# Output projections of the token mixers: the first two weight panels multiplied together, their last k tile at the end of both

## The reference, cut to what matters

```python
h = rmsnorm(x, g_norm1[l]) * (1.0 + mod[:, 1]) + mod[:, 0]
out, ctx_tensors = token_mixer(l, h, ctx)      # ends in: o.reshape(b, s, ...) @ w_o
x = x + mod[:, 2] * out
h = rmsnorm(x, g_norm2[l]) * (1.0 + mod[:, 4]) + mod[:, 3]
x = x + mod[:, 5] * swiglu(h, w_ffn_in[l], w_ffn_out[l])
```

## Time and profile before

| | |
|---|---|
| median of three timed runs | 3585.4 us |
| profiled execution, its own time | 3581.15 us |
| span of the profiled execution | 3579.3 us |
| TensorE matmuls busy | 3350.8 us (94%) |
| VectorE busy | 1886.4 us (53%) |
| ScalarE busy | 1123.7 us (31%) |
| mean granted TensorE clock | 0.950 of full speed |

### The profile page before, as it was taken

How to read it: one execution, slowest core, us unless ns; L and a number is a source line. 1 busy time by engine, 2 the same in 40 slices (tenths; PEclk the granted TensorE clock), 3 DMA queues, 4 the chain that set the end, 5 groups by cost and what they waited for, 6 DMA issues and landing times.

```text
span 3579.3 us, 53824 instructions
## 1 busy us (share of the span) xinstructions
PE 3350.8 (94%) x20800; PEld 3121.8 (87%) x20800; DVE 1886.4 (53%) x2732; ACT 1123.7 (31%) x1729; POOL 116.9 (3%) x72
## 2 busy tenths in 40 slices
PE   7899999999989998899999789989999897899999
PEld 7877789999987776799999666789999897899999
DVE  2333355767355665575853445566663687533333
ACT  2344423211134554321111333232111376321111
POOL 0211000000000000000000210000000000000000
PEclk6899998999999999899999899989999998999999
DMA  5211125343221110163522110143532221222222
GB/s 177 61 51 39 38 71 181 125 158 125 75 72 42 42 41 17 47 203 118 184 75 70 55 30 13 47 156 114 177 111 69 66 59 52 60 75 72 76 76 76
DMA packets 451128, 304.16 MB, mean 85 GB/s; under 512 B 12483, under 2 KB 430918, under 8 KB 451014
## 3 DMA queue, kind: packets, MB, share of 16 engines
q1 hardware_dynamic: 440676, 293.75, 26.8%
q10 hardware_dynamic: 10338, 8.88, 0.8%
HBM read 298.49 MB, written 4.10 MB: 85 GB/s over the span
## 4 chain that ended last, share of the span: by engine, by line
PE 85%; DVE 5%; ACT 5%; issue 2%; DVEq 1%; DMA 1%; ACTq 1%; SPq 0%
PE psB L309 30%; PE psA L309 30%; PE psD L309 8%; PE psC L372 3%; PE psA L353 2%; PE psC L325 2%; PE psC L364 2%; PE psB L353 2%; PE psD L826 2%; PE psA L811 1%; ACT h_hi L1459 1%; ACT work L1456 1%; ACTq L1458 1%; DVE work L2362 1%; PE psC L838 0%
## 5 line engine op out<-in xcount | busy, mean ns | idle before, releaser
L1477 ACT ACTIVATE w_hi<-raw 128x1024 fp32r<-128x1024 f32 (+1 forms) x309 | 319.4, 1035 | 1158.1 <-PE psB L309 770.5
L2011 DVE TENSOR_TENSOR w_lo<-raw,w_hi 128x1024 fp32r<-128x1024 f32 (+1 forms) x309 | 367.9, 1192 | 348.5 <-ACT w_hi L1477 348.2
L309 PE MATMUL psA<-h_hi,w_hi 128*128 128x320 f32 x1616 | 383.1, 319 | 46.8 <-DVE h_lo L2085 42.0
L309 PE MATMUL psB<-h_hi,w_hi 128*128 128x320 f32 x1616 | 371.4, 311 | 12.8 <-DVE w_lo L2369 12.8
L309 PE MATMUL psA<-h_lo,w_hi 128*128 128x320 f32 x1616 | 376.3, 315 | 0.0
L309 PE MATMUL psA<-h_hi,w_lo 128*128 128x320 f32 x1616 | 375.0, 314 | 0.0
L309 PE MATMUL psB<-h_lo,w_hi 128*128 128x320 f32 x1616 | 370.8, 311 | 0.0
L309 PE MATMUL psB<-h_hi,w_lo 128*128 128x320 f32 x1616 | 370.5, 311 | 0.0
L309 PEld LDWEIGHTS psA<-h_hi,w_hi 128*128 128x128 f32 x1616 | 274.5, 192 | 62.3 <-issue 32.2
L2041 DVE SCALAR_TENSOR_TENSOR work<-work,silu_c 128x1024 f32<-128x1024 f32 x252 | 312.6, 1282 | 11.7
L309 PEld LDWEIGHTS psB<-h_hi,w_hi 128*128 128x128 f32 x1616 | 272.6, 190 | 14.4 <-DVE w_lo L2369 14.4
(11 more groups left out here) (295 smaller groups left out, 5277.6 us busy)
## 6 DMA issues: line engine op xcount, KB each, us to landing
raw<-in_w_ffn_in SPq DMA_DIRECT2D x176, 512.0 KB, 3.9
work<-in_w_mod SPq DMA_DIRECT2D x144, 512.0 KB, 4.9
raw<-in_w_ffn_out SPq DMA_DIRECT2D x64, 512.0 KB, 4.0
raw<-in_w_ffn_out SPq DMA_DIRECT2D x32, 384.0 KB, 3.3
raw<-in_diff_w_in SPq DMA_DIRECT2D x24, 512.0 KB, 3.8
work<-in_w_mod SPq DMA_DIRECT2D x8, 1024.0 KB, 5.3
raw<-in_w_mod SPq DMA_DIRECT2D x16, 512.0 KB, 4.0
tables<-in_w_mod SPq DMA_DIRECT2D x16, 512.0 KB, 4.4
```

What stands on the lines that cost most here:

```text
L309: last = nc.tensor.matmul(out[:, b, 0:half], w[slot][:, kt * cols + c0:kt * cols + c0 + P], r[:, o:o + half], start=(kt == 0 and p == 0), ...
L1477: nc.scalar.activation(w_hi[s][:, 0:n], raw[s][:, 0:n], ACT.Copy).then_inc(hi_done, 1)
L2011: nc.vector.tensor_tensor(w_lo[s_][:, 0:n], raw[s_][:, 0:n], w_hi[s_][:, 0:n].bitcast(F32), ALU.subtract).then_inc(split_done, 1)
```

## The change

TensorE's instruction list changes in the four calls of `project` for the mixers' projections; the first turn is taken out of the loop and written as `first_pair`. It waits for the splits of both panels, multiplies k tiles 0 to 6 of panel 0 into psA, then k tiles 0 to 6 of panel 1 into psB, waits for the last head's output, and then multiplies k tile 7 of panel 0 and k tile 7 of panel 1. `gemm_done` is counted after each panel's last product, as before. The loop runs over the turns 1 to 3. The instruction lists of VectorE, ScalarE and SP stay as they are.

```diff
-            def project(name, kts, last_source, mod=None):
+            def project(name, kts, last_source, mod=None, mixer=False):
...
+                def first_pair():
+                    for j in range(2):
+                        assert take_panel(pe, name, 0, j) == j
+                    pe.wait_ge(x_done, base)
+                    for part in (range(kts - 1), range(kts - 1, kts)):
+                        if part[0]:
+                            last_source()
+                        for j in range(2):
+                            last = products(pe, psum[j], j, kts, P, 0, act_hi, act_lo, 0, T, TH, part)
+                            if part[0]:
+                                last.then_inc(gemm_done, 1)
+
                 if mod:
                     turn(0)
                     mod_turn(*mod, 2)
-                with pe.Fori(1 if mod else 0, KT // 2) as i:
+                if mixer:
+                    first_pair()
+                with pe.Fori(1 if mod or mixer else 0, KT // 2) as i:
                     turn(i)
...
-                project(f"wo{layer}", KT, lambda: mixed.wait_turns(pe, KT))
+                project(f"wo{layer}", KT, lambda: mixed.wait_turns(pe, KT), mixer=True)
```

## The result

The changed kernel takes 3609.7 us (median of five runs, 3608.43 to 3614.09) against 3585.4 us before on the same chip (five runs, 3583.77 to 3593.97): ratio 1.0065, 95% interval 1.005 to 1.008. It is slower by 24.3 us. Its profiled execution took 3610.07 us, 28.9 more than that of before.

The account below looks back on a forecast made before the run. TensorE, holding 85% of the chain that ended last, was taken to bound the kernel. 15.16 (stalls) + 1.22 (later starts) + 6.52 (clock) - 0.91 (gain) = +22.0 us, from 3585.4 to about 3607; range 3598.5 to 3613.

Parts of the forecast that it names:

- the gain: Fourth projection only: the wait before k tile 7 for the last block's low part goes, saving 0.91 us.
- The stall: Before panel 2 in each projection: TensorE waits 3.79 us for VectorE's `w_lo`, +15.16 us in all.
- Both splits first: Starts of second and fourth projection: 1.14 us later each, costing 0.61 us each at low clock, +1.22 us.
- rival C: Clock falls longer behind stalls (first half); later start delays the second projection's clock rise (second half); +27.3 us, 3613, chance 0.11.
- The clock: Behind each new stall: TensorE's clock falls, losing 1.63 us per stall, +6.52 us.
- Rival B: Behind the stalls: they occur but the clock stays up; +15.5 us, 3601, chance 0.16.
- D: Low-clock stretches behind norms and projection starts: the clock pays the stalls back; +4.2 us, 3590, no change, chance 0.05.

Follow-up runs that it names:

- two k tiles ahead: Changed kernel with only two of panel 1's k tiles before panel 0's last, panel 1's split awaited only ahead of panel 1: -4.2 us against before, ratio 0.9993.
- four k tiles left: Four of panel 1's k tiles drawn ahead of panel 0's last, four following, otherwise like the two-tile kernel; waits 0.98 to 0.99 us, one run only.
- the filler: Changed kernel plus 22 matmuls on unread data between the pair and panel 2 of each mixer's projection: +18.4 us against before, ratio 1.0051.
- the low part first: Changed kernel with VectorE making the next panel's low part after the addition, ahead of the squares, in every turn: +18.9 us against before, ratio 1.0049.
- the old order: Peeled first turn with panel 0 whole, then panel 1, but both splits awaited before the first matmul: +3.8 us against before, ratio 1.0007.
- the late split: Changed kernel with panel 1's split awaited only ahead of panel 1's first product: +15.6 us against before, ratio 1.0047.

## Why the prediction was right

*What bounds it, and the gain.* TensorE's idle time counted in full, and the waits that the change aimed at were covered in three of four places. The 0.91 us of the fourth were got back, also by the kernel with two k tiles ahead.

*The stall.* Forecast 3.79 us per projection from VectorE's 4.53, the 0.14 of the start and the 0.88 of cover. Counted as there, from one matmul's start to the next, it is 2309.38 less 2305.31 + 0.293, 3.78 us. As the profile counts idle time it is 3.62, since a matmul's record reaches 0.17 us past its successor's start. The order in VectorE's list (3.6 to 1.8 us) and the size of the cover (0.98 us with four k tiles left) show that this is the mechanism. One stall per projection and no second came, as argued. The term of 15.16 us was right to 0.1.

*Both splits first.* Forecast 0.61 us twice. In the fourth the later start was paid for as forecast: with the stall, 1.25 + 3.82 = 5.1 us against 3.79 + 1.63 + 0.61 - 0.91 = 5.1. In the second the start came 1.1 us later and the stretch behind it did not shrink by the half that the sum counted on, because the rise of the clock moved along. Counted as start and low clock together, against the first profile of before, this place cost 2.1 and 1.0 us in the two profiles of the changed kernel, 1.0 with the filler, 0.8 with the low part first and 2.0 with the old order. The term was undersized by 0.2 to 1.5 us there, by rival C's second half.

*The clock.* Forecast 1.63 us per stall. It fell behind every one of the 13 waits of 3.6 us in the four profiles that have them. The loss was 1.64 where it is read above, of which 0.11 are the first pair's (in the forecast's 1.63 too, by the same rows), and the filler took out 1.5. In two of the 13 it stayed low for longer and cost 2.7 and 2.5 us in place of 1.5, rival C's first half: the second projection of the first profile and the fourth of the kernel with the late split. Rival B did not occur. D was out too: no stall was paid back.

*The sum.* Forecast +22.0. The projections and their starts in the two profiles of the changed kernel give 5.4 + 1.1 + 7.5 + 5.4 + 1.3 + 3.8 = 24.5 and 5.4 + 1.1 + 5.3 + 5.4 + 1.3 + 3.8 = 22.3 us; timed it was +24.3 and +22.3. That these agree to 0.2 us is luck, and so in part is that the forecast lies within 2.3 us, since the interval of the first comparison spans 18 to 29 us. What remains of the first profile's 28.9 is more than covered by the GQA mixer's clock, which differs by 5 us between two profiles of the kernel before. What stays open is which share of the timed medians' last 2 us is clock in the projections and which elsewhere, since the timed runs have no stretches.

## What to carry to other kernels

Before taking k tiles of one panel behind those of another, count what lies between a buffer's release and its next use: here 48 matmuls became 6, while the other engines' chain from the one to the other needed 4.5 us. A wait that seems worth covering should first be found in the trace; three of these four did not exist, and two k tiles drawn ahead covered the fourth. When an engine's work for the next panel is queued behind bookkeeping, moving it forward helps only where nothing else waits for the bookkeeping, as the norm did in the last turn.

## What the runs showed of the hardware

A wait of TensorE can cost almost half its length again by the clock: behind 3.6 us the half-speed work that followed cost 1.5 us in 11 of 13 cases and 2.5 to 2.7 in the other two. Behind waits of 1.8 us between dense work the clock fell in two of eight (none of four in one profile, two of four in another), behind those of 0.98 us in none of four. Matmuls on unused data in the stall kept the clock at 1.00, but that kernel was still 18.4 us slower than the one without the stall. And two profiles of one kernel differed by 9.8 us in time with the same work, 5.1 of it in one attention mixer at another granted clock: a difference of a few us between single profiles has to be read from stretches that repeat.
